# Weight rests of a feed-forward product on one Trainium2 core: from VectorE subtractions to transfers that add

## The chip, the cores and the metric

The kernel runs on one core of a Trainium2 chip. The metric is the device time of one execution in microseconds (us). Times below are medians of several executions, or readings of one execution that was profiled. The engines are TensorE (PE; its weight loads are PEld), VectorE (DVE), ScalarE (ACT), GpSimd (POOL) and SyncE (SP); SP and POOL issue the transfers, and 16 DMA engines carry them out.

## The reference

One decoder layer in float32: a token mixer (a combined input projection, two gated linear recurrences, an output projection), then a feed-forward part. Only the feed-forward part matters here.

```python
def swiglu(h, w_ffn_in_l, w_ffn_out_l):
    a, u = jnp.split(h @ w_ffn_in_l, 2, axis=-1)
    return (jax.nn.silu(a) * u) @ w_ffn_out_l
# 576 tokens (512 + 64), D_MODEL = 1024, D_FF = 2816
```

## The kernel before

Matmuls run in the type fp32r, whose mantissa is shorter than float32's. To keep float32 accuracy every operand is split into a rounded part (`hi`) and a rest (`lo` = raw - hi), and a product is three matmuls: x_hi by w_lo, x_lo by w_hi, x_hi by w_hi.

The first feed-forward product works through `FT` = 22 pairs. A pair i is a block of 128 columns of the `a` half (u = 0) and the block of 128 columns of the `u` half (u = 1) that goes with it. A pair is computed by seven products `m1` to `m7` of half-sized operands (Strassen's scheme, Winograd's form) in place of eight, and each product is 12 matmuls of 128x288. On TensorE the order is that of `PAIR_ORDER`: from pair 2 on, `m1, m6, m7, m5, m2, m4, m3` for each pair.

The weights of a pair come in four groups. `g0` (both quarters of u = 0; products m1 and m2) and `g1` (one quarter of u = 1; product m3) are plain weights; they are three of the four plain quarters. `g3` (m6, m4) and `g2` (m5, m7) are sums of quarters, which `weight_sums` forms on DVE (L1496, L1499, L1501; semaphore `t_s`, three counts a pair). For each group ACT rounds the raw values into a `hi` buffer (`group_hi`, L1357) and DVE subtracts (`group_lo`, L1488) into the `lo` buffer. `g1` has one buffer, so `group_hi(i, "g1")` waits until m3 of pair i-1 is done; `g0`, `g2` and `g3` rotate through four slots, so `g0` of pair i+1 can be prepared during pair i. The first five groups (`FIRST`) are rounded on POOL.

The raw weights lie in two buffers (`w_raw_t` for odd pairs, part of `merged` for even ones). SP loads pair i+2 over pair i as soon as the last rest of pair i, that of `g1`, is there: `low_parts(sp, i - 2, "g1")` at L1262 to L1265, then two transfers of 512 KB (L1238). After the last pair the same wait stands ahead of the first two loads of the second product's weights (L1267 to L1270).

Each engine takes its queue in order. In a pair DVE's queue is: `upper_right(i-1)`, `group_lo(i, "g1")`, `weight_sums(i+1)`, `upper_sum(i)`, `group_lo(i+1, "g0")`, `lower_sum(i)`, `gated(i-1)`, `lower_right(i)`, `group_lo` of g3 and g2 of pair i+1, `lower_left(i)`. The five sums (L1596) add a product's bank to what stands in SBUF, and m2, m3 and m4 wait for such sums. ACT's queue is: `group_hi(i, "g1")`, `group_hi(i+1, "g0")`, `front(i)` (L1341), `gate(i-1)` (L1364), `group_hi(i+1, "g3")`, `corner(i)` (L1345), `group_hi(i+1, "g2")`. In the last pair the queues also hold the splits for the second product: `rows_hi` (ACT, L1422), `rows_lo` (DVE, L1625), `act_hi` and `act_lo`; on DVE `rows_lo(0)` and `act_lo(0)` stand ahead of `lower_right(21)`, for which m3(21) waits.

POOL has nothing to do between 676 us and the end.

Of the kernel before, what the change touches and what calls it, by code (L numbers as in the profile page):

```python
# [24 lines left out]
ALU = mybir.AluOpType  # L25
ACT = mybir.ActivationFunctionType
# [17 lines left out]
FT = FF // P  # L44
# [38 lines left out]
FIRST = {(0, "g2"): 1, (0, "g0"): 2, (0, "g3"): 3, (0, "g1"): 4, (1, "g0"): 5}  # L83
FIRST_GROUPS = len(FIRST)
# [44 lines left out]
def build(nc, x_prompt, x_sample, state_gla, state_hgrn, norm_mix_pre, norm_mix_post, norm_ffn_pre,  # L129
# [7 lines left out]
    def sem(name):  # L137
        return keep.enter_context(nc.semaphore(name))
# [91 lines left out]
    def rows(t):  # L230
        return t.rearrange("p k n -> p (k n)").rearrange("p (a n) -> p a n", a=2)

    def load_out(eng, u):
        half, kp = divmod(u - UB, KT // 2)
        eng.dma_start(rows(w_raw_t[:, u % NRAW, :, :]),
                      wout_v[:, 2 * kp:2 * kp + 2, half * HALF:(half + 1) * HALF]).then_inc(w_raw[u % NRAW], 16)
# [876 lines left out]
    def raw_pair(i):  # L1113
        return w_raw_t[:, :, :, :] if i % 2 == 1 else raw_even

    def ring(slot, hi):
        if slot < NSPL:
            return (w_hi_t if hi else w_lo_t)[:, slot, :, :]
        return (w2_hi if hi else w2_lo)[:, 0:KT, :]

    def group(i, g, hi):
        if g == "g1":
            return (w2_hi if hi else w2_lo)[:, KT:KT + 4, :]
        return ring(GSLOT[i, g], hi)

    def group_raw(i, g):
        if g == "g0":
            return raw_pair(i)[:, 0, :, :]
        if g == "g1":
            return raw_pair(i)[:, 1, 4:8, :]  # L1130
        first = 0 if g == "g2" else 2
        return w_sums[:, first:first + 2, :, :].rearrange("p s k n -> p (s k) n")

    def group_no(i, g):
        return 4 * i + GROUPS.index(g) + 1

    def bank(i, m):
        return ps[:, SET[i % 2][BANK[m]], 0:HT]

    def reused(i, g):  # L1140

        if g == "g1":
            return PRODUCT_NO[i - 1, "m3"] + 1
        mine = GOWNER[GSLOT[i, g]]
        before = mine[mine.index((i, g)) - 1]
        return max(PRODUCT_NO[before[0], m] for m, (x, b) in PRODUCTS.items() if GROUP_OF[b][0] == before[1]) + 1

    def low_parts(eng, i, g):

        if (i, g) in FIRST:  # L1150
            eng.wait_ge(first_lo, FIRST[i, g])
        else:
            eng.wait_ge(g_lo, group_no(i, g) - FIRST_GROUPS)

    m_half0 = work[:, 0:NT * HALF].rearrange("p (t n) -> p t n", t=NT)
    h_in = [sem(f"h_in{c}") for c in range(NT)]
# [14 lines left out]
    t_s = sem("t_s")  # L1171
    first_hi = sem("first_hi")
    g_hi = sem("g_hi")
    g_lo = sem("g_lo")
    a_hi = sem("a_hi")
    s_main = sem("s_main")
    x_free = sem("x_free")
# [57 lines left out]
    @block.sync  # L1235
    def _(sp):
        def load_pair(i, u, first):
            sp.dma_start(raw_pair(i)[:, u, :, :], wf1_v[:, :, first:first + P]).then_inc(pair_raw[i % 2], 16)  # L1238

        def load_rows(n):  # L1240
            half, kp = divmod(n, KPAIRS)
            sp.dma_start(rows(w_raw_t[:, n % NRAW, :, :]),
                         wf2_v[:, 2 * kp:2 * kp + 2, half * HALF:(half + 1) * HALF]).then_inc(d_raw[n % NRAW], 16)

        sp.wait_ge(m_lo, KT // 2)
        load_pair(0, 0, 0)
        load_pair(0, 1, FF)
        for u in range(UB + 5, UC):
            sp.wait_ge(w_lo, u)
            load_out(sp, u)  # L1250
            if u == UB + 5:
                sp.wait_ge(step_done, NO[G - 1, "o3"] + 1)
                sp.dma_start(g_post, norm_mix_post.partition_broadcast(P).rearrange("p o d -> p (o d)")).then_inc(g_post_in, 16)
        sp.wait_ge(st_out, 80 * G)
        for c in range(NT):
            sp.dma_start(h_t[0:tok(c), c, :], xp_v[c] if c < NC else xs_v).then_inc(h_in[c], 16)
        sp.dma_start(g_pre, norm_ffn_pre.partition_broadcast(P).rearrange("p o d -> p (o d)")).then_inc(g_pre_in, 16)
        sp.wait_ge(w_lo, UC)
        load_pair(1, 1, FF + P)
        sp.wait_ge(w_lo, UC + 1)  # L1260
        load_pair(1, 0, P)
        for i in range(2, FT):  # L1262
            low_parts(sp, i - 2, "g1")
            load_pair(i, 0, i * P)
            load_pair(i, 1, FF + i * P)  # L1265
        low_parts(sp, FT - 2, "g1")
        sp.dma_start(g_last, norm_ffn_post.partition_broadcast(P).rearrange("p o d -> p (o d)")).then_inc(g_in, 16)  # L1267
        low_parts(sp, FT - 1, "g1")
        load_rows(0)
        load_rows(1)  # L1270
        for n in range(2, ND):
            sp.wait_ge(d_lo, n - 1)
            load_rows(n)
        for i, t in enumerate(ORDER):
            n = tok(t)
            out = yp_v[t] if t < NC else ys_v
            sp.wait_ge(y_front, i + 1)
            sp.dma_start(out[:, 0:HALF], f_half[0:n, t, :]).then_inc(y_out, 16)
            sp.wait_ge(y_back, i + 1)
            sp.dma_start(out[:, HALF:D], f_back[t][0:n, :]).then_inc(y_out, 16)  # L1280
        sp.wait_ge(y_out, 2 * 16 * NT)

    @block.gpsimd
    def _(pool):
        for i, g in FIRST:
            if (i, g) == (0, "g0"):
                pool.wait_ge(unit_done, UB + 3)
            if (i, g) == (1, "g0"):
                pool.wait_ge(x_free, 2)
            pool.wait_ge(pair_raw[i % 2], 32)  # L1290
            if g == "g2":
                pool.wait_ge(t_s, 3)
            nc.gpsimd.tensor_copy(group(i, g, True), group_raw(i, g)).then_inc(first_hi, 1)

    @block.scalar
    def _(act):
# [40 lines left out]
        def front(i):  # L1337
            act.wait_ge(product, PRODUCT_NO[i, "m1"] + 1)
            if i >= 2:
                act.wait_ge(act_s, i - 1)  # L1340
            act.activation(fa[:, i % 2, HT:T], bank(i, "m1"), ACT.Copy).then_inc(m1_s, 1)  # L1341
# [9 lines left out]
        def group_hi(i, g):  # L1351
            act.wait_ge(product, reused(i, g))
            if g in ("g0", "g1"):
                act.wait_ge(pair_raw[i % 2], 32 * (i // 2 + 1))
            else:
                act.wait_ge(t_s, 3 * i + 3)
            act.activation(group(i, g, True), group_raw(i, g), ACT.Copy).then_inc(g_hi, 1)  # L1357

        def gate(i):
            act.wait_ge(c21_s, i + 1)  # L1360
            act.wait_ge(c11_s, i + 1)
            if i >= 1:
                act.wait_ge(act_s, i)
            act.activation(fs, fa[:, i % 2, :], ACT.Sigmoid).then_inc(sig_s, 1)  # L1364
# [36 lines left out]
        for i in range(FT - 1):  # L1401
            if i >= 1:
                group_hi(i, "g1")
                group_hi(i + 1, "g0")
            if i >= 2:
                front(i)
            if i == 1:
                act.preload_act_table_set("sigmoid_and_others")
            if i >= 1:
                gate(i - 1)  # L1410
            group_hi(i + 1, "g3")
            if i >= 2:
                corner(i)
            group_hi(i + 1, "g2")
# [18 lines left out]
                act.activation(act_tile(n, kk)[:, 0:T], a32[:, k, :], ACT.Copy).then_inc(k_hi, 1)  # L1433

        group_hi(FT - 1, "g1")
        front(FT - 1)
        gate(FT - 2)
        rows_hi(0)
# [40 lines left out]
    def _(dve):  # L1479
# [3 lines left out]
        def group_lo(i, g):  # L1483
            if (i, g) in FIRST:
                dve.wait_ge(first_hi, FIRST[i, g])
            else:
                dve.wait_ge(g_hi, group_no(i, g) - FIRST_GROUPS)
            dve.tensor_tensor(group(i, g, False), group_raw(i, g), group(i, g, True).bitcast(F32),  # L1488
                              ALU.subtract).then_inc(first_lo if (i, g) in FIRST else g_lo, 1)
# [153 lines left out]
        lower_left(0)  # L1643
        for i in range(1, FT):
            upper_right(i - 1)
            group_lo(i, "g1")
            if 1 < i < FT - 1:
                weight_sums(i + 1)
            upper_sum(i)
            if i == 1:  # L1650
                lower_sum(i)
            if i < FT - 1:
                group_lo(i + 1, "g0")
            if i == 1:
                lower_right(i)
                weight_sums(i + 1)
            else:
                lower_sum(i)
            gated(i - 1)
            if i == FT - 1:  # L1660
                rows_lo(0)
                act_lo(0)
            if i > 1:
                lower_right(i)
            if i < FT - 1:
                group_lo(i + 1, "g3")
                group_lo(i + 1, "g2")
            else:
                rows_lo(1)
                act_lo(1)  # L1670
            lower_left(i)
# [200 lines left out]
```

## Time and profile before

| | |
|---|---|
| median of 3 runs | 1082.92 us (1082.48 to 1083.53) |
| profiled execution | 1082.33 us, span of its instructions 1080.6 us |
| first feed-forward product, pairs 0 to 21 | from about 676 us to about 934 us of the span |
| PE busy over the span | 1059.2 us (98%) |
| DVE, ACT, POOL busy over the span | 686.5 us (64%), 483.4 us (45%), 71.7 us (7%) |

Times in the rows further down count from the span's start. The profiled execution lies outside its span by 1.7 us. In a window's row each engine has its busy time and the number of its instructions; a busy PE in a row means that matmuls follow each other without a gap. A row of the timeline has start, duration, engine, line, operation, operands; a bracket gives the idle time just before it and what ended that.

### The profile page before, as it was taken

What the parts mean: (1) busy time and instruction counts of PE and PEld (TensorE: products, weight loads), DVE (VectorE), ACT (ScalarE), POOL (GpSimd) and SP (SyncE); (2) the same over time, 40 slices, a digit from 0 to 9 for tenths busy, and PEclk for the clock granted to TensorE, in tenths of its full rate; (3) what the DMA queues carried; (4) which work ended last, traced back from release to release, by engine and by line L of the source; (5) the groups of instructions that cost most, each with busy time, mean ns of one, the idle gap of its engine ahead of it and who ended that gap; (6) DMA issues with size and microseconds to landing.
All of it is one profiled execution on the core that took longest, in us unless ns stands there. A gap on an engine that the chain in (4) does not pass through costs nothing.

```text
span 1080.6 us, 25224 instructions
## 1 busy us (share of the span) xinstructions
PE 1059.2 (98%) x11040; PEld 998.2 (92%) x11040; DVE 686.5 (64%) x1000; ACT 483.4 (45%) x772; POOL 71.7 (7%) x87
## 2 busy tenths in 40 slices
PE   7999999999999999999999999899999999999997
PEld 5999999999999999999999878789999999888886
DVE  6265643666435756436755479999999999834644
ACT  6433344632446433456325537644444444633532
POOL 5000003100013000031000011000000000000000
PEclk9999999999999999999999999999999999999999
DMA  7522223622225422236222283042423323322212
GB/s 190 165 72 79 68 72 95 189 61 75 74 61 177 107 71 79 70 98 176 61 80 69 61 276 85 1 117 79 114 82 94 102 80 98 122 93 79 78 59 87
DMA packets 138716, 105.30 MB, mean 97 GB/s; under 512 B 4016, under 2 KB 123824, under 8 KB 138608
## 3 DMA queue, kind: packets, MB, share of 16 engines
q1 hardware_dynamic: 133744, 85.88, 28.3%
q0 software_dynamic: 4864, 17.83, 5.4%
q8 instruction: 87, 1.43, 0.6%
q14 instruction: 21, 0.17, 0.1%
HBM read 91.89 MB, written 11.80 MB: 96 GB/s over the span
## 4 chain that ended last, share of the span: by engine, by line
PE 90%; DVE 5%; DVEq 2%; ACT 2%; issue 1%; ACTq 0%; DMA 0%; POOL 0%; SPq 0%; POOLq 0%
PE ps L256 43%; PE ps L1781 20%; PE ps L1805 13%; PE ps L1003 2%; PE ps L1070 2%; PE ps L366 2%; PE ps L1034 1%; PE ps L1024 1%; PE ps L980 1%; PE ps L1036 1%; PE ps L1041 1%; PE ps L1017 1%; PE ps L999 1%; PE ps L1061 0%; DVE work L1596 0%
## 5 line engine op out<-in xcount | busy, mean ns | idle before, releaser
L256 PE MATMUL ps<-x_hi,w_lo_t 128*128 128x288 f32 x1152 | 251.6, 300 | 0.0
L256 PE MATMUL ps<-x_hi,w_hi_t 128*128 128x288 f32 x1152 | 246.5, 296 | 0.0
L256 PE MATMUL ps<-x_lo,w_hi_t 128*128 128x288 f32 x1152 | 245.9, 295 | 0.0
L242 ACT ACTIVATE w_hi_t<-w_raw_t 128x1024 fp32r<-128x1024 f32 x73 | 77.3, 1058 | 313.7 <-PE ps L256 313.1
L246 DVE TENSOR_TENSOR w_lo_t<-w_raw_t,w_hi_t 128x1024 fp32r<-128x1024 f32 x73 | 89.3, 1223 | 168.7 <-ACT w_hi_t L242 168.7
L256 PEld LDWEIGHTS ps<-x_hi,w_lo_t 128*128 128x128 f32 x1152 | 184.2, 189 | 5.1 <-issue 3.5
L256 PEld LDWEIGHTS ps<-x_lo,w_hi_t 128*128 128x128 f32 x1152 | 185.2, 188 | 0.0
L256 PEld LDWEIGHTS ps<-x_hi,w_hi_t 128*128 128x128 f32 x1152 | 185.1, 188 | 0.0
L1781 PE MATMUL ps<-x_hi,w_lo_t 128*128 128x288 f32 x264 | 78.6, 298 | 3.6 <-DVE work L1596 2.4
L1781 PE MATMUL ps<-x_hi,w_hi_t 128*128 128x288 f32 x264 | 78.3, 297 | 0.0
L1781 PE MATMUL ps<-x_lo,w_hi_t 128*128 128x288 f32 x264 | 78.3, 296 | 0.0
L1357 ACT ACTIVATE w_hi_t<-merged 128x1024 fp32r<-128x1024 f32 x41 | 43.1, 1054 | 57.0 <-PE ps L1781 49.2
L789 DVE TENSOR_TENSOR Q<-Q,B 128x768 f32<-128x768 f32 (+1 forms) x24 | 23.8, 992 | 69.4 <-PE ps L1003 30.2
L1596 DVE TENSOR_TENSOR work<-work,ps 128x288 f32<-128x288 f32 x110 | 49.7, 452 | 12.2 <-PE ps L1781 7.8
L1805 PE MATMUL ps<-w_hi_t,x_hi 128*128 128x512 f32 x180 | 57.1, 389 | 0.0
L1488 DVE TENSOR_TENSOR w_lo_t<-merged,w_hi_t 128x1024 fp32r<-128x1024 f32 x43 | 53.5, 1250 | 0.8
L1781 PEld LDWEIGHTS ps<-x_hi,w_lo_t 128*128 128x128 f32 x264 | 49.8, 189 | 4.3 <-issue 1.7
L1781 PEld LDWEIGHTS ps<-x_hi,w_hi_t 128*128 128x128 f32 x264 | 50.1, 190 | 0.0
L1781 PEld LDWEIGHTS ps<-x_lo,w_hi_t 128*128 128x128 f32 x264 | 50.0, 189 | 0.0
L1625 DVE TENSOR_TENSOR w_lo_t<-w_raw_t,w_hi_t 128x1024 fp32r<-128x1024 f32 x17 | 20.8, 1224 | 44.0 <-ACT w_hi_t L1422 44.0
L1422 ACT ACTIVATE w_hi_t<-w_raw_t 128x1024 fp32r<-128x1024 f32 x17 | 18.0, 1059 | 54.7 <-PE ps L1805 50.4
L1781 PE MATMUL ps<-xe_hi,w_lo 128*128 128x288 f32 x136 | 40.5, 298 | 0.8 <-DVE work L1596 0.8
(305 smaller groups left out, 2141.0 us busy)
## 6 DMA issues: line engine op xcount, KB each, us to landing
w_raw_t<-in_w_in_dram SPq DMA_DIRECT2D x73, 512.0 KB, 3.8
merged<-in_w_ffn_in_dram SPq DMA_DIRECT2D x22, 512.0 KB, 5.3
w_raw_t<-in_w_ffn_in_dram SPq DMA_DIRECT2D x22, 512.0 KB, 4.7
w_raw_t<-in_w_ffn_out_dram SPq DMA_DIRECT2D x22, 512.0 KB, 3.6
h_t<-in_x_prompt_dram SPq DMA_DIRECT2D x8, 512.0 KB, 5.9
h_t<-in_state_gla_dram POOLq DMA_DIRECT2D x4, 1024.0 KB, 6.3
h_t<-in_state_hgrn_dram POOLq DMA_DIRECT2D x8, 512.0 KB, 8.7
out_dram<-h_t POOLq DMA_DIRECT2D x4, 1024.0 KB, 5.4
```

The source lines that it names most:

```text
L242: nc.scalar.activation(w_hi_t[:, u % NSPL, 0:nk, :], w_raw_t[:, u % NRAW, 0:nk, :], ACT.Copy).then_inc(w_hi, 1)
L246: nc.vector.tensor_tensor(w_lo_t[:, u % NSPL, 0:nk, :], w_raw_t[:, u % NRAW, 0:nk, :], w_hi_t[:, u % NSPL, 0:nk, :].bitcast(F32), ALU.subt ...
L256: m = nc.tensor.matmul(out[:, q, :], w[:, u % NSPL, k, :], x(k, q), start=first and i == 0, stop=last and i == len(todo) - 1)
L366: ins = pe.matmul(out_bank(half, c), x[:, k, cols], w[:, kk, :], start=first and i == 0, stop=last and i == 2, skip_group_check=True)
L789: dve.tensor_tensor(qf, qf, first.broadcast_to(shape), ALU.mult)
L1003: m = nc.tensor.matmul(s[t:t + STRIP, o + t // 2:o + (t + STRIP) // 2], K[:, h, c * C + t:c * C + t + STRIP], second(Q[:, h, c * C + t:c * ...
L1070: m = nc.tensor.matmul(s[:, o:o + v.shape[-1]], kblk[(0, 0, 1, 2)[i]][first:first + 32, b, :], v, start=True, stop=True)
L1357: act.activation(group(i, g, True), group_raw(i, g), ACT.Copy).then_inc(g_hi, 1)
L1488: dve.tensor_tensor(group(i, g, False), group_raw(i, g), group(i, g, True).bitcast(F32), ALU.subtract).then_inc(first_lo if (i, g) in FIRS ...
L1596: return dve.tensor_tensor(out, term, bank(i, m), ALU.add)
L1781: ins = nc.tensor.matmul(bank(i, m), w[:, k0 + k, :], xx[:, k, :], start=(k == 0 and n == 0 and m in STARTS), stop=(k == 3 and n == 2), sk ...
L1805: m = nc.tensor.matmul(f_bank(half, t), x, w, start=first and i == 0, stop=last and i == len(todo) - 1)
```

## The change

For `g0` of pairs 2 to 21 and `g1` of pairs 1 to 21 DVE's subtraction is taken out. ACT writes the negated rounded value into the `lo` buffer (`group_neg`: the same rounding as `group_hi`, with scale -1), and POOL then issues a transfer from the raw buffer to the `lo` buffer that adds what it carries to what stands there (`add_raw`, `accum_op=ALU.add`). Both lie in SBUF. The counts of its landing (`raw_lo`, 16 a transfer) are what PE and SP wait for. SP's wait ahead of the loads of pair i covers the landing of both transfers of pair i-2 and its weight sums.

```diff
+    def by_transfer(i, g):
+        return (i, g) not in FIRST and g in ("g0", "g1")
+    def nth(i, g):
+        return i - 1 if g == "g0" else i
...
+        elif by_transfer(i, g):
+            eng.wait_ge(raw_lo[g], 16 * nth(i, g))
         else:
-            eng.wait_ge(g_lo, group_no(i, g) - FIRST_GROUPS)
+            eng.wait_ge(g_lo, 2 * (i - 1) + (1 if g == "g3" else 2))
...
         for i in range(2, FT):
+            if i > 2:
+                low_parts(sp, i - 2, "g0")
+                sp.wait_ge(t_s, 3 * (i - 2) + 3)
             low_parts(sp, i - 2, "g1")
             load_pair(i, 0, i * P)
             load_pair(i, 1, FF + i * P)
+        low_parts(sp, FT - 2, "g0")
         low_parts(sp, FT - 2, "g1")
+        sp.wait_ge(t_s, 3 * FT)
...
+        low_parts(sp, FT - 1, "g0")
         low_parts(sp, FT - 1, "g1")
         load_rows(0)
         load_rows(1)
...
+        def add_raw(i, g):
+            pool.wait_ge(g_neg[g], nth(i, g))
+            if nth(i, g) > 1:
+                pool.wait_ge(raw_lo[g], 16 * (nth(i, g) - 1))
+            pool.dma_start(group(i, g, False), group_raw(i, g), accum_op=ALU.add).then_inc(raw_lo[g], 16)
+        for i in range(1, FT):
+            add_raw(i, "g1")
+            if i + 1 < FT:
+                add_raw(i + 1, "g0")
...
+        def group_neg(i, g):
+            act.activation(group(i, g, False), group_raw(i, g), ACT.Copy, scale=-1.0).then_inc(g_neg[g], 1)
...
             if i >= 1:
                 group_hi(i, "g1")
+                group_neg(i, "g1")
                 group_hi(i + 1, "g0")
             if i >= 2:
                 front(i)
+            if i >= 1:
+                group_neg(i + 1, "g0")
...
         group_hi(FT - 1, "g1")
+        group_neg(FT - 1, "g1")
...
             upper_right(i - 1)
-            group_lo(i, "g1")
...
-            if i < FT - 1:
-                group_lo(i + 1, "g0")
```

ACT's queue in pair 8, which is the pair whose rows are shown below; `w_hi<-merged` is g1 of pair 8, `w_hi_t<-w_raw_t` is g0 of pair 9, `work<-ps` is `front(8)`, `work<-work` is `gate(7)`. Before:

```order
L1357 ACTIVATE w_hi<-merged 128x512 [waits pair_raw0,product]
L1357 ACTIVATE w_hi_t<-w_raw_t 128x1024 [waits pair_raw1,product]
L1341 ACTIVATE work<-ps 128x288 [waits act_s,product]
L1364 ACTIVATE work<-work 128x576 [waits act_s,c11_s,c21_s]
L1357 ACTIVATE w_hi<-merged 128x1024 [waits t_s,product]
```

And with the change:

```order
L1384 ACTIVATE w_hi<-merged 128x512 [waits pair_raw0,product]
L1387 ACTIVATE w_lo<-merged 128x512
L1384 ACTIVATE w_hi_t<-w_raw_t 128x1024 [waits pair_raw1,product]
L1368 ACTIVATE work<-ps 128x288 [waits act_s,product]
L1387 ACTIVATE w_lo_t<-w_raw_t 128x1024
L1394 ACTIVATE work<-work 128x576 [waits act_s,c11_s,c21_s]
```

The negated copy of g1 stands ahead of the rounding of g0, and that of g0 behind `front` and ahead of `gate`.

SP's queue at the end of the pairs: the loads of pair 21, a gain vector, and the first rows of the second product's weights. Before:

```order
L1238 DMA w_raw_t<-in_w_ffn_in_dram 128x8x128 [waits g_lo]
L1238 DMA w_raw_t<-in_w_ffn_in_dram 128x8x128
L1267 DMA merged<-in_norm_ffn_post_dram 128x1024 [waits g_lo]
L1242 DMA w_raw_t<-in_w_ffn_out_dram 128x2x512 [waits g_lo]
L1242 DMA w_raw_t<-in_w_ffn_out_dram 128x2x512
```

And with the change:

```order
L1248 DMA w_raw_t<-in_w_ffn_in_dram 128x8x128 [waits g1_lo,t_s,g0_lo]
L1248 DMA w_raw_t<-in_w_ffn_in_dram 128x8x128
L1282 DMA merged<-in_norm_ffn_post_dram 128x1024 [waits t_s,g1_lo,g0_lo]
L1252 DMA w_raw_t<-in_w_ffn_out_dram 128x2x512 [waits g1_lo,g0_lo]
L1252 DMA w_raw_t<-in_w_ffn_out_dram 128x2x512
```

The same transfers in the same order; what they wait for is now the landing of other transfers.

## Rows read from the trace of the kernel before

**Rows 1.** Windows: us; then busy of PE, PEld, DVE, ACT, POOL; clock; DMA; GB/s.

```profile
683.00:686.00 3.00, 1.50 (x15) 1.20 (x14) 3.00 (x3) 1.27 (x3) 0.00 (x0) 1.00 0.00 0
686.00:689.00 3.00, 3.00 (x14) 2.88 (x15) 2.01 (x5) 2.01 (x3) 0.00 (x0) 0.56 0.00 0
...
711.00:722.00 11.00, 9.92 (x73) 9.51 (x72) 10.46 (x15) 3.88 (x7) 0.00 (x0) 1.00 0.36 97
...
755.00:766.00 11.00, 11.00 (x85) 11.00 (x84) 10.09 (x15) 5.00 (x7) 0.00 (x0) 1.00 0.35 95
```

**Rows 2.** Timeline of PE: all idle stretches of at least 0.1 us after 697 us.

```profile
710.43 0.40 PE L1781 MATMUL ps<-xe_hi,w_lo_t 128*128 128x288 f32 x1 [1.21 <-DVE w_lo_t L1488]
...
717.92 0.38 PE L1781 MATMUL ps<-x_hi,w_lo_t 128*128 128x288 f32 x1 [0.86 <-DVE work L1596]
...
719.96 0.37 PE L1781 MATMUL ps<-xe_hi,w_lo 128*128 128x288 f32 x1 [0.22 <-DVE work L1596]
...
932.50 0.37 PE L1781 MATMUL ps<-xe_hi,w_lo 128*128 128x288 f32 x1 [0.53 <-DVE work L1596]
```

**Rows 3.** Timeline of pair 8 from its first matmul, and ACT's first of pair 9.

```profile
777.34 0.30 PE L1781 MATMUL ps<-x_hi,w_lo_t 128*128 128x288 f32 x1
...
777.54 0.63 ACT L1357 ACTIVATE w_hi<-merged 128x512 fp32r<-128x512 f32 x1 [1.82 <-PE ps L1781]
...
778.07 1.04 ACT L1357 ACTIVATE w_hi_t<-w_raw_t 128x1024 fp32r<-128x1024 f32 x1
...
778.20 0.69 DVE L1488 TENSOR_TENSOR w_lo<-merged,w_hi 128x512 fp32r<-128x512 f32 x1 [0.21 <-ACT w_hi L1357]
...
778.92 0.99 SPq L1238 DMA_DIRECT2D merged<-in_w_ffn_in_dram  x2
...
779.14 0.41 ACT L1341 ACTIVATE work<-ps 128x288 f32<-128x288 f32 x1
...
788.69 0.63 ACT L1357 ACTIVATE w_hi<-w_raw_t 128x512 fp32r<-128x512 f32 x1 [1.84 <-PE ps L1781]
```

**Rows 4.** These two loads: time to landing, and the window of their data.

```profile
DMA to landing us min/median/max: 3.9/4.5/5.2
...
779.50:784.00 4.50, 4.50 (x37) 4.50 (x36) 4.22 (x7) 0.71 (x3) 0.00 (x0) 1.00 0.86 233
```

**Rows 5.** The page's DMA issues: stores that POOL issues, median us to landing.

```profile
out_dram<-h_t POOLq DMA_DIRECT2D x4, 1024.0 KB, 5.4
out_dram<-h_t POOLq DMA_DIRECT2D x8, 512.0 KB, 3.8
```

**Rows 6.** DMA from 174 to 182 us, one such store beside a load.

```profile
q0 software_dynamic: 272, 1.05, 37.6%
...
out_dram<-h_t POOLq DMA_DIRECT2D x1, 1024.0 KB, 6.0
w_raw_t<-in_w_in_dram SPq DMA_DIRECT2D x1, 512.0 KB, 4.6
```

**Rows 7.** Timeline of pair 1: ACT's rounding of g0 of pair 2, SP's load.

```profile
700.24 1.04 ACT L1357 ACTIVATE w_hi_t<-merged 128x1024 fp32r<-128x1024 f32 x1
...
701.51 1.56 SPq L1238 DMA_DIRECT2D w_raw_t<-in_w_ffn_in_dram  x2
```

**Rows 8.** Timeline of pair 21, the last.

```profile
922.45 0.63 ACT L1357 ACTIVATE w_hi<-w_raw_t 128x512 fp32r<-128x512 f32 x1 [1.84 <-PE ps L1781]
...
923.83 39.02 SPq L1242 DMA_DIRECT2D w_raw_t<-in_w_ffn_out_dram  x10
...
927.61 1.06 ACT L1422 ACTIVATE w_hi_t<-w_raw_t 128x1024 fp32r<-128x1024 f32 x1 [2.57 <-DMA w_raw_t<-in_w_ffn_out_dram]
...
929.11 1.22 DVE L1625 TENSOR_TENSOR w_lo_t<-w_raw_t,w_hi_t 128x1024 fp32r<-128x1024 f32 x1
...
931.90 0.46 DVE L1596 TENSOR_TENSOR work<-work,ps 128x288 f32<-128x288 f32 x1
```

More of the change, by code:

```diff
@@ L1174, in build @@
     g_lo = sem("g_lo")
+    g_neg = {"g0": sem("g0_neg"), "g1": sem("g1_neg")}
+    raw_lo = {"g0": sem("g0_lo"), "g1": sem("g1_lo")}
     a_hi = sem("a_hi")
```

## The prediction, as it was made before the changed kernel ran

> **What bounds the kernel now.** I read the busy shares by window first. In the steady pairs PE is busy for all of 11.00 us and DVE for 10.09 of it; ACT has 5.00 and POOL none [rows 1]. So DVE is nearly full, but PE sets the time: it has no gap. Then the timeline of PE. After 697 us it idles four times: 1.21, 0.86 and 0.22 us in pair 2 and 0.53 us before m3 of the last pair, 2.82 us together [rows 2]. That is all that a lighter DVE could ever give back in this stage. A pair takes 788.69 - 777.54 = 11.15 us [rows 3], so a product takes 1.59 us. The question is therefore not what DVE gains but whether the new chain (negate, transfer, landing) keeps its dates.
>
> **What goes and what comes.** DVE loses per pair one subtraction of 0.69 us [rows 3] and one of twice the size (1.22 us, the duration of the same operation on 128x1024 in the last pair [rows 8]): 1.9 of some 10.1 us. From pair 3 on it hides under PE and is worth nothing. ACT gains two copies a pair, 0.63 and 1.04 us (priced as the roundings of the same sizes [rows 3]): 5.0 becomes 6.7 us of 11.15, no bound. POOL issues two transfers a pair; it is idle otherwise. Nothing is queued behind its waits but the next such transfer.
>
> **The price of a transfer that adds.** The trace has none. Nearest are stores issued by POOL: 512 KB in 3.8 us, 1024 KB in 5.4 us from issue to landing [rows 5], which makes 2.2 us fixed and 1.6 us per 512 KB. By the queue's share the 16 engines spend 37.6% of 8 us, 3.0 us, on 1 MB [rows 6], so 1.5 us per 512 KB. A transfer that adds must read two sources. Low end: it costs what a copy does, 1.6 us per 512 KB. High end: nothing in the trace limits it; I take four times, 6 us. I choose twice, 3.0 to 3.2 us, since two reads stand against one. Then g0 (512 KB) lands D0 = 5.4 us after its issue and g1 (256 KB) D1 = 3.8 us after. The Trainium skill, "Collectives: The Full Stack", section "The bandwidth ceiling: the fold count and why AG ≠ RS ≠ AR", says that an adding transfer moves half of what a copy does because both reads go through one ring, and gives 31 GB/s per engine for a copy; an estimate from that page is 2.1 us per 512 KB, with which the sum would be that of the cheap rival below.
>
> **The circuit of two pairs.** g0 of pair i+2 needs its raw weights; SP now loads these only after g1's transfer of pair i has landed. Counted from the first matmul of pair i (777.34 in pair 8 [rows 3]):
> - rounding of g1 starts at 0.20, the next ACT operation could start at 0.73; the negated copy fills 0.73 to 1.36;
> - D1 = 3.8: landed at 5.2. There SP issues the loads, 3.6 us later than the 1.58 us (778.92) of before [rows 3];
> - the loads take 5.2 us alone to the second's landing, and 0.86 of 4.5 us = 3.9 us of all 16 engines [rows 4];
> - ACT then rounds g0 (1.04), runs `front` (0.41, occupying 0.31) and negates g0 (1.04): 2.4 us;
> - D0 = 5.4.
>
> Sum 1.36 + 3.8 + 5.2 + 2.4 + 5.4 = 18.2 us, against 22.3 us for two pairs. If nothing met, the chain would hold. But the load and the g0 transfer of the next pair run at the same time on the same 16 engines. Where a store met a load in the trace, the store took 6.0 us instead of 5.4 [rows 5, 6]. With the adding transfer served first, the load is later by its 3.0 us and D0 by 0.6: 21.8 us, just inside 22.3. With equal shares D0 is later by 3.0 as well: 24.2 us, 12.1 per pair. The middle is 23.0, so 11.5 per pair: **+0.35 us** for each of the last 18 pairs, **+6.3 us**, between 0 and +17.
>
> **The start.** In pair 1 ACT would round g0 of pair 2 at 700.24 [rows 7]; with g1's negation ahead it runs from 700.8, and its own negation ends at 702.8. Landing at 708.2. m1(2) started at 710.43 - 1.21 - 1.59 = 707.6, m6(2) at 710.43 [rows 2]. m6(2) waits for g3's rest, which comes behind weight sums and `gated(0)` and not behind a removed subtraction that mattered (PE's m5(1) held DVE there), so it stays at 710.4 and swallows the 0.6 us. The 0.86 and 0.22 us go, since one or two subtractions less stand ahead of those sums: -1.1. But the load of pair 3, issued at 701.51 before [rows 7], is now issued when g1 of pair 1 has landed, 700.8 + 3.8 = 704.6; beside D0 it lands 5.2 to 8.2 us later, at most 712.8, and g0 of pair 3 at 720.6 to 723.6. Before, m1(3) started at 719.96 + 1.59 = 721.5. I take 722.4: **+0.9 us** in all, between -1.1 and +2.1.
>
> **The end.** g1 of pair 21: rounding at 922.45, negation done at 923.6, landed at 927.4. SP issues the first rows of the second product there, not at 923.83; they landed 3.8 us after the issue (ACT waited for them until 927.61) [rows 8], so ACT starts at 931.2. On DVE `rows_lo(0)` (929.11) and `act_lo(0)` stand ahead of `lower_right(21)` (931.90) [rows 8], for which m3(21) waits. They shift to 932.3 and, the 2.8 us between them unchanged, to 935.1, so m3(21) starts at 935.7 instead of 932.50: **+3.2 us**; with a g1 transfer at a copy's price (3.0 us) +2.4. PE is busy to the end after that, so nothing gives it back.
>
> **Sum:** 6.3 + 0.9 + 3.2 = +10.4 us on the profiled execution of 1082.33, 1092.7. The median of the runs lies 0.6 us above that execution: **1093.3 us**. Own range of this case: 1086 to 1105.
>
> **Rivals.**
> - **Cheap transfers** (up to 2.3 us of the engines per 512 KB). Two pairs need 1.36 + 3.3 + 7.4 + 2.4 + 4.9 = 19.4 us, the circuit holds. Start -1.1, end +2.4 to +3.0: +1.3 to +1.9, **1084.5 us**, within 0.2%. For it: no row shows that adding costs more than reading twice, and transfers inside SBUF may be faster than stores to memory.
> - **Dear transfers**, slower by much. At three times a copy (4.5 us): D1 = 4.5, the load 5.2 + 4.5, D0 = 6.7 when served first and 11.2 with equal shares: 24.7 to 29.2 us for two pairs, middle 26.9, +2.3 per pair, +41; end +3.9, start +4: **1132 us**. At four times: 28.4 us or more, +55 and up, 1150. It decides once a 512 KB transfer takes more than some 3.5 us of the engines; a longer issue on POOL counts likewise. It would also make PE wait over 2 us in each pair. The one place where PE stood still for half of 3 us was followed by a granted clock of 0.56 [rows 1]; such gaps would add to this case.
> - **A gain.** If the landing came as early as DVE's rest does now (778.9 in pair 8), the four waits of 2.82 us would go: 1080.1 us. Against it: even a copy of 512 KB takes 3.8 us, and the end loses 2.4.
> - **The adding transfer is cut into small pieces**, so that it is not one row of 4 KB per partition: then it is the dear case.
>
> **Chances.** Forecast 0.40, cheap 0.24, dear 0.32, gain 0.04. A measurement here can tell about 0.2%, 2.2 us, from no change: faster 0.04, same 0.24, slower 0.72. The range runs from 1083 (cheap end) to 1150; it leaves out the gain and the far part of the dear case, some 0.16.
>
> **What would show it.** Rows for m1 of pairs 3 to 21 with an idle time before them, ended by a DMA, of 0.3 to 2 us; SP's loads 3.6 us later in each pair; software-queue work of some 4.5 us per pair on the engines; ACT waiting for raw weights; m3(21) with over 3 us of idle time. PE without gaps in pairs 4 to 20 would prove the cheap case; pairs of over 12.5 us the dear one. A transfer rate other than twice a copy's is what would make the prediction wrong.

## The result, and the profile of the changed kernel

The changed kernel takes **1106.81 us** (median of 4 runs, 1103.78 to 1111.31), the kernel before 1082.70 in the runs beside it: 1.0224 times as long (95% interval 1.0202 to 1.0245), **+24.1 us**. The forecast was 1093.3 us, +10.4. The profiled execution took 1103.99 us, +21.7 against that of before; its span is 1102.0 us, +21.4. The traces can account for these 21.4 us; the median of the runs lies 2.8 us above the profiled execution.

The page of the changed kernel. Busy us by engine; in part 3 the packets, MB and share of the queue that POOL feeds:

```profile
PE 1065.4 (97%) x11040; PEld 1002.8 (91%) x11040; DVE 652.6 (59%) x959; ACT 513.2 (47%) x813; POOL 107.3 (10%) x128
...
q0 software_dynamic: 10768, 33.82, 13.8%
...
PE 69%; issue 13%; DMA 9%; DVE 4%; ACT 2%; POOL 1%; DVEq 1%; ACTq 1%; SPq 0%; POOLq 0%
```

DVE has lost 33.9 us of work and ACT gained 29.8. No engine became the bound. What is new is the DMA in the chain that ended last (third line: 9%, where the kernel before has 0%), and PE shows where. Its timeline from 697 us on, idle stretches of at least 0.25 us (to be held against [rows 2]):

```profile
708.33 0.40 PE L1812 MATMUL ps<-x_hi,w_lo_t 128*128 128x288 f32 x1 [1.08 <-DMA w_lo_t<-merged]
...
723.88 0.61 PE L1812 MATMUL ps<-x_hi,w_lo 128*128 128x288 f32 x1 [4.10 <-DMA w_lo<-w_raw_t]
...
771.59 0.40 PE L1812 MATMUL ps<-x_hi,w_lo 128*128 128x288 f32 x1 [1.36 <-DMA w_lo<-w_raw_t]
...
805.73 0.40 PE L1812 MATMUL ps<-x_hi,w_lo_t 128*128 128x288 f32 x1 [0.27 <-DMA w_lo_t<-merged]
...
831.84 0.40 PE L1812 MATMUL ps<-x_hi,w_lo_t 128*128 128x288 f32 x1 [3.56 <-DMA w_lo_t<-merged]
...
868.00 0.41 PE L1812 MATMUL ps<-x_hi,w_lo 128*128 128x288 f32 x1 [0.91 <-DMA w_lo<-w_raw_t]
...
880.63 0.40 PE L1812 MATMUL ps<-x_hi,w_lo_t 128*128 128x288 f32 x1 [1.23 <-DMA w_lo_t<-merged]
...
915.25 0.40 PE L1812 MATMUL ps<-x_hi,w_lo 128*128 128x288 f32 x1 [0.91 <-DMA w_lo<-w_raw_t]
...
927.90 0.40 PE L1812 MATMUL ps<-x_hi,w_lo_t 128*128 128x288 f32 x1 [1.26 <-DMA w_lo_t<-merged]
...
952.41 0.49 PE L1812 MATMUL ps<-xe_hi,w_lo 128*128 128x288 f32 x1 [3.54 <-DVE work L1630]
```

The nine rows ended by a DMA are each the first matmul of a pair (m1), which waits for g0's transfer. The tenth is m3 of the last pair.

Three windows behind the three largest idle stretches, and for comparison one behind a stretch of 1.36 us (columns as in [rows 1]):

```profile
723.80:727.20 3.40, 3.32 (x14) 3.33 (x15) 2.61 (x3) 1.09 (x2) 0.00 (x0) 0.50 0.26 63
833.00:836.40 3.40, 3.40 (x17) 3.40 (x16) 1.75 (x3) 2.19 (x4) 0.59 (x1) 0.51 0.52 152
952.50:955.90 3.40, 3.40 (x14) 3.30 (x15) 3.06 (x7) 2.07 (x4) 0.00 (x0) 0.50 0.64 196
771.70:775.10 3.40, 3.40 (x26) 3.40 (x27) 1.91 (x2) 1.94 (x3) 0.86 (x1) 1.00 0.63 129
```

After 4.10, 3.56 and 3.54 us without a matmul the granted clock is 0.5, so 1.2 GHz, for 3.4 us (in the second case from 1.2 us after PE had resumed): 14 to 17 matmuls fit where 26 do at 2.4 GHz. In time that is 1.2 to 1.6 us for each (a matmul takes 0.13 us here); the pairs behind the first two took 12.72 and 12.78 us instead of 11.15. Before, there was one such stretch in this part of the program, at 686 us [rows 1], and it is still there.

**Where the 21.4 us are.**

| part of the span | forecast | measured |
|---|---|---|
| start: first matmul of pair 3, from 721.63 to 723.88 | +0.9 | +2.25 |
| from there to that of pair 21, 18 pairs: 200.62 to 215.27 | +6.3 | +14.65 |
| from there to m3 of pair 21: 10.25 to 13.26 | +3.2 | +3.0 |
| behind it (half clock) | 0 | +1.5 |

The 14.65 us are 9.5 us in the seven idle stretches between 771 and 928, 3.2 us in the two pairs that began at or fell into half clock, and 2 us in small pieces (behind each wait a pair lost some 0.2 us more than its bracket).

The DMA issues from 740 to 920 us (size and median time to landing) show what the transfers cost, here of the changed kernel:

```profile
q0 software_dynamic: 4431, 11.99, 39.7%
...
merged<-in_w_ffn_in_dram SPq DMA_DIRECT2D x16, 512.0 KB, 6.7
w_raw_t<-in_w_ffn_in_dram SPq DMA_DIRECT2D x16, 512.0 KB, 6.8
w_lo_t<-merged POOLq DMA_DIRECT2D x8, 512.0 KB, 6.9
w_lo_t<-w_raw_t POOLq DMA_DIRECT2D x4, 512.0 KB, 5.6
w_lo<-w_raw_t POOLq DMA_DIRECT2D x8, 256.0 KB, 3.3
w_lo<-w_raw_t POOLq DMA_DIRECT2D x4, 512.0 KB, 7.1
```

g1's transfer (256 KB) lands in 3.3 us. The loads, 4.6 and 4.8 us before in the same window, now take 6.7 and 6.8, and g0's transfer (512 KB) 5.6 to 7.1. Two transfers of one circuit meet and both take longer. The experiments ask whether that, and nothing else, is the loss.

### The profile page after: what moved, and what is told of

Same layout as the page of the kernel before. It is cut to its first block, busy times and chain, and to the rows that moved or that the text cites. A ratio compares the mean times of both kernels' runs of the same rounds, so it can differ in the third digit from the quotient of the medians.

```text
span 1102.0 us, 25325 instructions
## 1 busy us (share of the span) xinstructions
PE 1065.4 (97%) x11040; PEld 1002.8 (91%) x11040; DVE 652.6 (59%) x959; ACT 513.2 (47%) x813; POOL 107.3 (10%) x128
## 4 chain that ended last, share of the span: by engine, by line
PE 69%; issue 13%; DMA 9%; DVE 4%; ACT 2%; POOL 1%; DVEq 1%; ACTq 1%; SPq 0%; POOLq 0%
PE ps L256 42%; PE ps L1836 13%; DMA w_lo<-w_raw_t 3%; DMA w_raw_t<-in_w_ffn_in_dram 3%; PE ps L1003 2%; PE ps L1070 2%; PE ps L366 2%; DMA w_lo<-merged 1%; PE ps L1034 1%; PE ps L1024 1%; PE ps L980 1%; PE ps L1036 1%; PE ps L1041 1%; DMA w_lo_t<-merged 1%; PE ps L1812 1%
## 5 line engine op out<-in xcount | busy, mean ns | idle before, releaser
L1812 PE MATMUL ps<-x_hi,w_lo_t 128*128 128x288 f32 x264 | 79.1, 300 | 10.1 <-DMA w_lo_t<-merged 7.4
L1522 DVE TENSOR_TENSOR w_lo_t<-merged,w_hi_t 128x1024 fp32r<-128x1024 f32 x33 | 41.3, 1261 | 8.7 <-ACT w_hi_t L1384 8.5
```

The source lines that it names most:

```text
L1812: ins = nc.tensor.matmul(bank(i, m), w[:, k0 + k, :], xx[:, k, :], start=(k == 0 and n == 0 and m in STARTS), stop=(k == 3 and n == 2), sk ...
```

## The experiments

My theory is the circuit of the prediction: g1's transfer lands, only then SP loads, the load meets the next g0's transfer, and that one lands after PE wants it. Rivals: each adding transfer has a price of its own, wherever it stands; the late load alone is what costs; the losses are only those at the start and the end. Where a kernel leaves a group to DVE, `group_lo` for it stands where it stood before, and the counts of the waits follow. All kernels were timed beside the kernel before (median 1082.2 to 1082.8 us).

### One group alone

```diff
-        return (i, g) not in FIRST and g in ("g0", "g1")
+        return (i, g) not in FIRST and g == "g1"      # e1_g1_only
+        return (i, g) not in FIRST and g == "g0"      # e2_g0_only
```

> Only g1's rests come from adding transfers, g0's are subtracted on DVE as before. Theory M (the loss between pairs comes from the 512 KB transfer of g0 and the load of the next raw weights meeting on the DMA engines): no g0 transfer, so the load is later by some 3.5 us but takes its 5.2 us again and lands in time; all pairs from 4 to 20 take 11.15 us, no m1 waits. Left are the end (m3 of the last pair waits 3 to 3.5 us) and at most one stretch at half clock behind it: 1085 to 1087 us. Rival L (the late load by itself is what costs) and rival P (each adding transfer costs something, whatever it meets): waits stay in the pairs, 1092 us or more.

> Only g0's rests come from adding transfers, g1's are subtracted on DVE, so SP issues the loads 1.6 us into a pair as before and ahead of g0's transfer. Theory M: g0's transfer stands behind the load in nearly every pair and takes 7.5 to 9 us instead of 5.5; it is needed 7.7 us after its issue, so m1 waits 0 to 1.5 us in most pairs: 1086 to 1100 us, the end as before (0.5 us). Rival L: with the load early again nothing waits, 1081 to 1084 us.

With g1 alone: 1086.35 us (9 runs), 1.0032 (1.0023 to 1.0042). With g0 alone: 1083.6 us (10 runs), 1.0008 (0.9998 to 1.0017). Neither comes near the loss of both. In both kernels PE runs pairs 4 to 20 without a wait of over 0.1 us. First the idle row and two windows at the end of the kernel with g1, then, after 697 us, the only idle row of over 1 us of the kernel with g0:

```profile
934.43 0.58 PE L1824 MATMUL ps<-xe_hi,w_lo 128*128 128x288 f32 x1 [3.62 <-DVE work L1638]
...
932.80:936.20 3.40, 1.77 (x7) 1.80 (x8) 3.31 (x9) 2.07 (x5) 0.00 (x0) 0.50 0.46 159
936.20:939.60 3.40, 3.40 (x13) 2.92 (x12) 2.97 (x6) 3.38 (x5) 0.00 (x0) 0.50 0.48 154
```

```profile
710.10 0.40 PE L1824 MATMUL ps<-x_hi,w_lo_t 128*128 128x288 f32 x1 [2.53 <-DMA w_lo_t<-merged]
```

The loss with g1 is that of the last pair alone: 3.62 us before m3(21), and twice 3.4 us at half clock. With g0 alone what is left is pair 2: its g0 lands late once, and from 711.5 to 714.9 the granted clock is 0.50. I had expected waits in most pairs from the meeting of load and transfer. That failed. Here DVE frees the raw buffer early, as before, so the load starts 1.8 us ahead of g0's transfer (780.46 and 782.28), and both land in time, with medians of 4.7 us for the load and 6.2 to 6.5 us for g0. A transfer of 6.3 us behind an early load is harmless.

### The ends taken out

```diff
+        return (i, g) not in FIRST and g == "g0" and i > 2          # e7_g0_from_3
+        return (i, g) not in FIRST and g == "g1" and i < FT - 1     # e9_g1_to_20
+        ... and g in ("g0", "g1") and (i, g) != (FT - 1, "g1")      # e3_last_subtracted
```

> Only g0 from pair 3 on comes from transfers; g0 of pair 2 and all g1 are subtracted on DVE. That takes away the 2.5 us wait at m1 of pair 2 that the kernel with all g0 by transfer had, and the half clock behind it, and keeps the lighter DVE in pair 2 (waits of 0.86 and 0.22 us there). Expected 1.1 us under the kernel before if g0 of pair 3 lands in time, 1081.6 us; if it meets the load issued beside it, m1 of pair 3 waits 0.7 us: 1082.3 us.

> Only g1 of pairs 1 to 20 comes from transfers; g1 of the last pair and all g0 are subtracted on DVE. With all g1 by transfer the pairs were clean and the end lost 3.1 us and 3.4 us of half clock. If that was all due to the last pair's transfer, what is left is the gain in pair 2 (0.86 us of waits became 0.26): 1082.0 us, 4 us under that kernel.

> The change as it is, but g1 of the last pair is subtracted on DVE, so that the first rows of the second product are loaded as early as before. If the end term is right (3.0 us at m3 of the last pair, and 1.6 us of half clock behind that gap) the gap there is 0.5 us again and the median is 4 to 5 us under that of the changed kernel, 1102 us. If the gap stays, the wait there is for something else.

- g0 from pair 3 on: 1081.59 us (11 runs), 0.9992 (0.9983 to 1.0001).
- g1 up to pair 20: 1081.84 us (11 runs), 0.9996 (0.9988 to 1.0005). The 3.7 us by which g1 alone was over the kernel before were those of the last pair.
- The change without g1 of pair 21: 1101.49 us (5 runs, 1091.01 to 1104.14), 1.0185 (1.0168 to 1.0202): 5.3 us less than the change, where the end's 3.0 and the 1.5 of half clock behind it would make 4.5; the spread of both kernels is larger than the difference from that. The row of m3(21) is what shows it: its idle time is back at that of [rows 2]:

```profile
941.18 0.37 PE L1824 MATMUL ps<-xe_hi,w_lo 128*128 128x288 f32 x1 [0.53 <-DVE work L1638]
```

The kernel with g0 from pair 3 is the fastest of those that leave nothing out, and its interval still holds 1: the measurement does not tell it from the kernel before.

### Both in the middle, and each with a cheaper transfer

```diff
+        return (i, g) not in FIRST and ((g == "g0" and i > 2)
+                                        or (g == "g1" and i < FT - 1))   # e10
...
-            pool.dma_start(..., accum_op=ALU.add)
+            pool.dma_start(...)                     # e11: for g1; e12: for g0
```

> Only the two parts that cost nothing by themselves are put together: g0 by transfer from pair 3 on, g1 by transfer up to pair 20; pair 2's g0 and pair 21's g1 are subtracted on DVE. Circuit theory: the two were free only because one end of the circuit was missing (with g0 alone the load is issued early and g0's transfer starts 1.4 us behind it; with g1 alone nothing meets the load). Together the load waits for g1's transfer and then meets g0's, so most of the 14.65 us of pairs 3 to 21 come back, without the start and the end: 1090 to 1098 us, PE waiting 1 to 4 us for g0's landing in every second to fourth pair. Additive theory (each transfer has a price of its own, and what was lost were the start, the end and disturbances): the differences of the two kernels add up, -0.6 and -0.4, so 1081 to 1083 us.

> As the kernel with both parts in the middle, but the transfer of g1 only copies (the addition to g1's rest is left out; the values of one quarter are then wrong in scale, the work is not otherwise changed). It should land 2.3 instead of 3.3 us after its issue, so the load goes out 1 us earlier. Circuit theory: 1.36 + 2.3 + about 8.4 for the load beside g0's transfer + 2.4 + 7 to 8 = 21.5 to 22.5 us for two pairs against 22.3, about balanced: most of the loss goes, 1082 to 1089 us. If the loss came only from the load and g0's transfer meeting, whatever their date: as with both adding, 1090 to 1098 us.

> As the kernel with both parts in the middle, but the transfer of g0 only copies (the addition to g0's rest is left out). The engines' work of g0's transfer falls from 2.6 to 1.4 us. Circuit theory: the load takes 8.4 - 1.2 = 7.2 us and g0 lands 5.5 to 6 us after its issue; 1.36 + 3.3 + 7.2 + 2.4 + 5.8 = 20.1 us, the circuit holds with over 2 us to spare: 1081.5 to 1083.5 us, no wait of PE for g0. If the late load itself were what costs (issued 3.6 us later than before because of g1's transfer, which adds here as in the change), the loss would stay: above 1088 us.

| kernel | us | ratio (95%) |
|---|---|---|
| only g0 (pairs 3 to 21) | 1081.59 | 0.9992 (0.9983 to 1.0001) |
| only g1 (pairs 1 to 20) | 1081.84 | 0.9996 (0.9988 to 1.0005) |
| both | 1100.25 | 1.0153 (1.0131 to 1.0176) |
| both, g1 only copied | 1093.85 | 1.0109 (1.0092 to 1.0126) |
| both, g0 only copied | 1081.09 | 0.9986 (0.9976 to 0.9995) |

This is the deciding table. Two parts that cost nothing one by one cost 17.5 us together, so the price is not that of a transfer but that of the circuit. (By the circuit I had expected 1090 to 1098 us for both, by a price for each transfer 1081 to 1083.) When g1's transfer is shortened by 1.0 us (2.3 instead of 3.3 to landing), 6.4 us of it go. I had expected 1082 to 1089; the result lies in the 1090 to 1098 that I had given to the rival by which only the meeting counts, whatever its date. But that rival meant no change against the kernel with both, and 6.4 us are gone: so the date counts too, by less than I thought. When g0's transfer is shortened all of it goes, although g1's adding transfer is unchanged and still holds back the load: a load that is late by g1's transfer alone does not cost anything. This kernel, which leaves the addition to g0's rest out, is even 1.7 us under the kernel before, clear of the noise; in its trace the waits of 0.86 and 0.22 us in pair 2 [rows 2] are gone. The DMA issues of that kernel from 740 to 920 us:

```profile
q0 software_dynamic: 4608, 12.58, 30.0%
...
w_raw_t<-in_w_ffn_in_dram SPq DMA_DIRECT2D x16, 512.0 KB, 5.3
...
w_lo_t<-merged POOLq DMA_DIRECT2D x8, 512.0 KB, 3.6
w_lo<-w_raw_t POOLq DMA_DIRECT2D x8, 256.0 KB, 3.3
```

The same queue needs 30.0% of the engines, against 38.5% with both adding, and the loads land in 5.3 instead of 6.8 us: where they met, the adding transfer had slowed them.

The kernel with both shows one turn of the circuit in full. Timeline rows from pair 7 to the first matmul of pair 9, ACT, POOL, SP and PE in order of time; `w_raw_t` is the buffer of odd pairs:

```profile
770.94 0.62 ACT L1395 ACTIVATE w_lo<-w_raw_t 128x512 fp32r<-128x512 f32 x1
...
772.03 0.86 POOL L1321 DMA_DIRECT2D w_lo<-w_raw_t  x1 [8.29 <-ACT w_lo L1395]
...
775.40 1.02 SPq L1252 DMA_DIRECT2D w_raw_t<-in_w_ffn_in_dram  x2
...
784.11 1.06 ACT L1390 ACTIVATE w_hi_t<-w_raw_t 128x1024 fp32r<-128x1024 f32 x1 [1.43 <-DMA w_raw_t<-in_w_ffn_in_dram]
...
785.36 1.05 ACT L1395 ACTIVATE w_lo_t<-w_raw_t 128x1024 fp32r<-128x1024 f32 x1
...
786.28 0.99 SPq L1252 DMA_DIRECT2D merged<-in_w_ffn_in_dram  x2
...
786.71 0.86 POOL L1321 DMA_DIRECT2D w_lo_t<-w_raw_t  x1 [2.88 <-ACT w_lo_t L1395]
...
796.12 0.61 PE L1824 MATMUL ps<-x_hi,w_lo_t 128*128 128x288 f32 x1 [3.49 <-DMA w_lo_t<-w_raw_t]
```

and the landings of the two loads and of g0's transfer, both issued between 786 and 788 us:

```profile
DMA to landing us min/median/max: 4.4/7.0/9.6
...
w_lo_t<-w_raw_t POOLq DMA_DIRECT2D x1, 512.0 KB, 9.4
```

The first matmul of pair 7 started at 770.20. From there to the load's issue 5.2 us; from it until ACT could round, 8.7; to POOL's issue, 2.6; to the landing, 9.4. That is 25.9 us, against 22.3 for two pairs, and PE stood still for 3.49. (0.13 us of the difference lie outside the bracket.) Here the load (786.28) went out 0.43 us ahead of g0's transfer (786.71). One pair earlier the transfer (774.90) was 0.5 us ahead of the load (775.40). The same two views there:

```profile
DMA to landing us min/median/max: 7.0/7.6/8.2
...
w_lo_t<-merged POOLq DMA_DIRECT2D x1, 512.0 KB, 5.9
```

There only the load is slow (with g0 alone its median is 4.7); in the turn before, the second of the two loads took 9.6 us and g0's transfer was slow as well. One turn of each does not prove a rule, so here are all turns of three kernels (the change, the change without g1 of pair 21, and this one). "Load" is the time from SP's first issue to the landing of the second transfer; medians, with the range in brackets:

| issue of the load against that of g0's transfer | turns | g0, us | load, us |
|---|---|---|---|
| 0.4 to 1.9 us behind | 24 | 5.8 (5.2 to 6.2) | 8.4 (6.8 to 9.6) |
| 0.3 us behind to 0.1 us ahead | 13 | 7.1 (6.7 to 7.5) | 8.7 (8.4 to 10.0) |
| 0.3 to 0.7 us ahead | 11 | 8.3 (7.8 to 9.5) | 8.7 (6.2 to 10.1) |
| 1.2 to 1.5 us ahead | 5 | 7.1 (6.7 to 7.8) | 5.8 (5.7 to 8.8) |
| 2.5 to 3.6 us ahead | 3 | 4.5 (4.5 to 5.6) | 5.6 (5.6 to 5.8) |

So the load is late unless it is issued about a microsecond or more ahead, and with the order of two issues, half a microsecond apart, goes whether g0's transfer is late too. It also says how near to balance the circuit is. If g0's transfer were first in every turn, two pairs would by these rows take 5.2 + 8.4 + 2.6 + 5.8 = 22.0 us, just inside 22.3 (an estimate); with the load first by half a microsecond in every turn they would take 5.2 + 8.7 + 2.6 + 8.3 = 24.8.

### The addition taken out everywhere

```diff
-            pool.dma_start(group(i, g, False), group_raw(i, g), accum_op=ALU.add).then_inc(raw_lo[g], 16)
+            pool.dma_start(group(i, g, False), group_raw(i, g)).then_inc(raw_lo[g], 16)
```

> The change with transfers that copy instead of adding (the rests are then wrong; only the addition is left out). It prices the addition alone. The changed kernel's packets of 4 KB took 327 ns and its g0 transfers 5.5 us when nothing met them. If the second read is what makes them long, copies take some 190 ns per packet and 3.8 to 4.2 us, the circuit of load and transfer has over 3 us to spare and no m1 waits after pair 3; left are the end (2.5 to 3 us) and a stretch at half clock: 1085 to 1088 us. If an adding packet costs no more than a copied one, nothing changes: 1103 to 1111 us.

1084.7 us (8 runs), 1.002 (1.001 to 1.003), just under the range that I had expected. All pairs from 3 on take 11.15 us. In the window of 740 to 920 us q0 carries 12.58 MB with 22.9% of the engines' time:

```profile
q0 software_dynamic: 4609, 12.58, 22.9%
```

That is 180 x 0.229 / 24 = 1.72 us for each 512 KB (12.58 MB are 24 of them); in the changed kernel 180 x 0.397 x 0.524 / 11.99 = 3.12 us. A transfer that adds costs 1.8 times a copy in this stage.

### Two attempts to give the two an order

```diff
             low_parts(sp, i - 2, "g1")
+            if i > 2:
+                sp.wait_ge(g_neg["g0"], nth(i - 1, "g0"))   # e4_load_behind_g0
+                low_parts(sp, i - 1, "g0")                  # e6_load_after_g0
             load_pair(i, 0, i * P)
```

> The change as it is, but SP issues the loads of pair i only when ACT has negated g0 of pair i-1, so that g0's transfer goes ahead of the load or nearly so in every pair. Theory M with order (whichever of the two is issued first is served whole, the other waits; 5.4 to 5.9 us for g0 when it is 0.8 us or more ahead, 8 to 9.5 us when it is 0.3 us behind): no g0 transfer over 7.5 us, fewer and shorter waits at m1, 1090 to 1098 us. Rival W (the engines' work for the additions is too much in any order): as the changed kernel, 1103 to 1111 us.

> The change, but SP issues the loads of pair i+2 only when g0's transfer of pair i+1 has landed, so that the two never meet (in the fourth experiment both were released by the same event and SP's went out 0.2 us ahead of POOL's). Theory M: g0's transfers all take 5.4 to 5.6 us and the loads 5.2; the circuit is 1.4 + 2.5 + 5.5 + 5.2 + 2.4 + 5.5 = 22.5 us against 22.3, so 0.1 to 0.3 us per pair; with start, end and half clock 1091 to 1096 us, although the raw weights are there 4 us later than in the changed kernel when nothing meets. Rival L (a late load is what costs, meeting or not): more than the changed kernel, 1112 us and up.

The first, 1108.67 us (4 runs), 1.0246 (1.0221 to 1.027), gave no order: where SP and POOL are released by the same negation, in ten of nineteen turns, SP is quicker by 0.2 us (836.31 against 836.52 in one pair). From 740 to 920 us g0's transfers have medians of 6.9 to 7.8 us, against 5.6 to 7.1 with the change. The time lies in the range that I had given to rival W, but the order that was to tell the two apart did not come about; in those ten turns g0's transfer took 7.8 to 9.5 us. The run is inconclusive on what a real order would bring.

The second, 1127.53 us (4 runs), 1.0416 (1.0402 to 1.0431), does separate the two. g0's transfer is alone:

```profile
q0 software_dynamic: 144, 0.52, 61.5%
...
w_lo_t<-w_raw_t POOLq DMA_DIRECT2D x1, 512.0 KB, 4.5
```

(window 742.96 to 747.46 us, so 0.615 x 4.5 = 2.8 us of 16 engines, 4.5 us to landing). But the load is too late for all else, and PE waits three times a pair, and for g0's landing only twice in the whole stage (at 844.06 and 968.20); the first of these products comes again at 754.86, so this pair took 13.0 us:

```profile
741.86 0.37 PE L1814 MATMUL ps<-x_hi,w_lo_t 128*128 128x288 f32 x1 [0.41 <-ACT work L1370]
...
744.15 0.37 PE L1814 MATMUL ps<-x_hi,w_lo_t 128*128 128x288 f32 x1 [0.46 <-DVE work L1632]
...
746.20 0.37 PE L1814 MATMUL ps<-xe_hi,w_lo 128*128 128x288 f32 x1 [0.22 <-DVE work L1632]
```

ACT and DVE take their queues in order. ACT's rounding of g0 waits for the raw weights with `front` behind it, and DVE's weight sums wait with `lower_right` and the others behind them:

```profile
DVE merged L1532 <- DMA w_raw_t<-in_w_ffn_in_dram: 34.3, 7, 7.9
...
ACT w_hi_t L1386 <- DMA merged<-in_w_ffn_in_dram: 31.1, 7, 5.5
```

(waits from 735 to 930 us: total, times, longest.) I had expected 1091 to 1096 us and was wrong by over 30. Rival L had it right here (1112 us and up): a load that is late by a whole transfer more costs by itself, while one late by g1's transfer alone did not.

## Why the prediction was right or wrong, point by point

**Right.** PE sets the time and DVE's relief is worth nothing: DVE lost 33.9 us. The shape of the loss was named: m1 waits for g0's landing, SP's load is later by the time of g1's transfer, m3(21) waits over 3 us. The end came out at 3.0 us for a forecast of 3.2, and by its own steps. ACT, SP and DVE in pair 21 of the changed kernel, against [rows 8]:

```profile
939.89 0.62 ACT L1387 ACTIVATE w_lo<-w_raw_t 128x512 fp32r<-128x512 f32 x1
...
944.11 6.53 SPq L1252 DMA_DIRECT2D w_raw_t<-in_w_ffn_out_dram  x3
...
947.92 1.06 ACT L1455 ACTIVATE w_hi_t<-w_raw_t 128x1024 fp32r<-128x1024 f32 x1 [5.99 <-DMA w_raw_t<-in_w_ffn_out_dram]
...
951.81 0.45 DVE L1630 TENSOR_TENSOR work<-work,ps 128x288 f32<-128x288 f32 x1
```

From the pair's first matmul (939.15) the load is issued after 4.96 us (forecast 5.15), its rows are there 3.8 later (forecast 3.8), and DVE's sum follows. No adding transfer meets a load here, and there the forecast held.

**The price of the transfer.** The 3.0 to 3.2 us of the engines per 512 KB, twice a copy, was near: 2.8 us alone, 3.1 in the stage. The times to landing were chosen too long, D0 = 5.4 and D1 = 3.8; alone they are 4.5 and 3.3. The sum left out that POOL issues a transfer some time after the negation has ended: in the turn above g1's at 772.03, 0.5 us later than the sum has it, and g0's after 2.6 us for the sum's 2.4. So the 5.2 us to the load's issue came true by two errors that cancel. Had the circuit met nothing it would have been 5.2 + 5.2 + 2.6 + 4.5 = 17.5 us long. The Trainium skill, "Collectives: The Full Stack", section "The bandwidth ceiling: the fold count and why AG ≠ RS ≠ AR", has the adding transfer at half a copy's rate; the traces agree in the ratio (1.8), while the estimate of 2.1 us from its figure is below the 2.8 us measured. Why the ratio is what it is, no run here shows.

**The step that failed** is the +0.35 us a pair. It was the middle between a circuit of 21.8 us (the adding transfer served first) and one of 24.2 (equal shares). There was no reason in the rows for the middle, and each end was a case that this kernel runs through: where g0's transfer was issued first it took 5.9 us, where the load was, 9.4. Even the dearer end was not the worst: the turn above took 25.9 us, with the load needing 8.7 us to be of use (8.2 in the dear end) and g0 9.4 (8.4). Over 18 pairs the changed kernel took 215.27 us, less 3.2 for the clock: 23.6 us for two pairs, 0.63 us a pair over 11.15, nearer to the dear end. The term is then 18 x 0.63 = 11.4 us for the 6.3 forecast. It lay inside the bounds of 0 to 17 that the text gave. On the profiled execution the forecast is short by 11.0 us: 5.1 of this term, 4.7 of the clock and 1.4 of the start, both below, less 0.2 at the end.

A wait does not come in each pair. After pair 3 there were seven, of 0.27 to 3.56 us, and the next came one to four pairs after the last. That a wait gives the circuit slack, which the next turns use up, fits this but is argued. I had forecast 0.3 to 2 us in each pair; what came was nothing for some pairs and then up to 3.6. This matters because of the next point.

**Left out: the clock.** I had kept the half-clock stretches for the dear rival, where PE would wait over 2 us in each pair. Three single gaps of 3.5 to 4.1 us were enough for 4.7 us, 3.2 in the pairs and 1.5 behind the end. The row that could have warned was cited: at 686 us a stretch of 3 us of which PE stood still for half was followed by half clock [rows 1]. The forecast's own wait before m3(21), 3.2 + 0.53 = 3.7 us, is longer than that, so the main case should have carried it.

**The start** was +2.25 instead of +0.9. g0 of pair 2 landed as forecast (m1(2) started at 708.33, forecast 708.2): it was issued 1.5 us ahead of the load of pair 3 and took 5.6 us, near the 5.4 that the forecast had for a transfer alone. That is in part luck, since alone it would be 4.5. g0 of pair 3 was issued 0.4 us behind a load and took 9.4 us: m1(3) started at 723.88, just past the dear end of the 720.6 to 723.6 by the text, which took 722.4.

**The rivals.** "Cheap" was the right answer for a transfer at a copy's price: it forecast 1084.5, and the kernel with plain copies took 1084.7. That it fits so closely is luck in part: its end cost 1.9 us and not 2.4 to 3.0, and behind it came 1.5 us of half clock, which the rival did not have. And the transfer was not cheap. "Dear" decided at 3.5 us of the engines, which was not reached; its time of 1132 us was far off, but half clock behind the waits, which only this rival spoke of, came. What no rival said is that neither of the two groups costs anything alone.

**What stays open.** Why half a microsecond of order matters so much in the engines or their queues was not settled; the table of turns shows only that it does. Not tried was a kernel that lets g0's transfer go ahead of the load by half a microsecond or more in every pair, without making the load later than that; by the 22.0 us above it would just hold. The runs of the kernels with both groups spread wide (1091.01 to 1104.14 with g1 of pair 21 on DVE). The turns of one execution differ in which of the two is first, which would fit, but that the executions differ in it is only argued: each kernel has one trace.

## What to carry to other kernels

Moving work from an engine that is full but not the bound to the DMA queues bought nothing here and added a landing to a chain that had slack. Follow the buffer around its whole circuit (last reader, load, rounding, transfer, product), add up the times to landing as they are *beside* the other transfers of the circuit, and take the dear end when the two are issued within half a microsecond of each other or the load is just ahead. If the sum then comes near the period, each part of the change may be free alone and both together not; and a late chain may pay in few large gaps, behind which the clock adds its own share.

## What the runs showed of the hardware

- A transfer from SBUF to SBUF that adds float32 takes 2.8 us of the 16 engines per 512 KB, and lands 4.5 us after its issue; 256 KB land in 3.3 us. As plain copies 256 KB landed in 2.3 us; 512 KB landed in 3.5 to 3.6 us where they were issued some 1.1 us ahead of a load (medians, g0 only copied) and in 4.0 to 5.1 where they were mostly issued 0.15 us ahead of it (all copied). POOL's rows show 0.86 us for the issue of one.
- Two transfers that meet do not share in the same way in each order. With g0's adding transfer issued 0.5 us first it landed in 5.9 us, and the load's median went from 4.7 to 7.6; issued 0.4 us behind the load it took 9.4 in one turn, and 7.8 to 9.5 in the eleven such turns of the table.
- Gaps of 3.5 to 4.1 us on PE were each followed by a granted clock of 0.5 for 3.4 us; with g1 alone (3.62 us) and with both groups in the middle (3.49 us) it began inside the gap and lasted 6.8. That of 1.36 us was not. Between them the length of the gap does not tell. In the kernel with both groups in the middle the first two of these windows lie behind 2.35 and 2.60 us without a matmul; the third, of the kernel in which g1 is only copied, begins 1.3 us after a gap of only 1.79 us (columns as in [rows 1]):

```profile
746.30:749.70 3.40, 3.40 (x16) 3.40 (x17) 1.62 (x3) 0.80 (x3) 0.00 (x0) 0.59 0.46 80
...
881.60:885.00 3.40, 3.38 (x25) 3.38 (x26) 2.19 (x3) 2.18 (x4) 0.00 (x0) 1.00 0.47 84
...
898.75:902.15 3.40, 3.40 (x16) 3.40 (x16) 1.89 (x3) 2.32 (x4) 0.86 (x1) 0.50 0.41 115
```
